# Forgetting attention reordered: head pairs begun among the key tiles, two heads' values side by side, gates copied raw, turned tiles in full banks, norm sums in four groups

## The reference

```python
proj = h @ w_in                                   # h: normed x, (512, 1024)
u_glu, q, k, v, f_logit, gate_c, gate_a = split(proj)
u = depthwise_conv31(a * sigmoid(gate)) + dw_b    # 512 channels, from u_glu
conv_out = silu(layernorm(u, ln_g, ln_b)) @ pw_w
logf = log_sigmoid(f_logit + fox_bf)              # (512, 8)
c = cumsum(logf)                                  # per head
s = q @ k.T / 8 + c_i - c_j ; causal mask         # per head, 512 x 512
attn = softmax(s) @ v                             # 8 heads
merged = sigmoid(gate_c) * conv_out + sigmoid(gate_a) * (attn @ attn_branch_w)
x = x + merged @ w_out
```

## Time and profile before

| what | value |
|---|---|
| median of three runs | 1825.19 us (1824.74 to 1825.5) |
| span of the profiled execution | 1825.3 us |
| PE busy in it | 1712.9 us (94%) |
| VectorE, ScalarE busy | 721.0 us, 409.8 us |
| queries to `pw` (1148.80 to 1347.61 us) | 198.81 us, PE busy 184.50, mean granted clock 0.93 |
| one round of a pair (1269.00 to 1299.72 us) | 30.72 us |

### The profile page before, as it was taken

How to read it: one execution, slowest core, us unless ns; L and a number is a source line. 1 busy time by engine, 2 the same in 40 slices (tenths; PEclk the granted TensorE clock), 3 DMA queues, 4 the chain that set the end, 5 groups by cost and what they waited for, 6 DMA issues and landing times. The chain is left out here.

```text
span 1825.3 us, 21471 instructions
## 1 busy us (share of the span) xinstructions
PE 1712.9 (94%) x8587; PEld 960.1 (53%) x8587; DVE 721.0 (40%) x1329; ACT 409.8 (22%) x758; POOL 21.9 (1%) x29
## 2 busy tenths in 40 slices
PE   6998999999999999999999899998899999877987
PEld 4575466568876443444434334443368674453542
DVE  4635424666545011101110229925353424351425
ACT  5112113532123010110100040126531013220112
POOL 0000000000000000000000000000000000000001
PEclk9998999999999999999999999998999999988999
DMA  9411275111325999999999912210112222269974
GB/s 364 154 57 46 71 261 199 46 70 47 138 93 217 418 419 422 427 420 419 420 426 421 382 69 92 92 46 1 46 47 92 93 99 109 81 253 376 327 270 173
DMA packets 88935, 374.35 MB, mean 205 GB/s; under 512 B 9797, under 2 KB 10133, under 8 KB 73749
## 3 DMA queue, kind: packets, MB, share of 16 engines
q1 hardware_dynamic: 82084, 350.14, 49.0%
q10 hardware_dynamic: 3712, 12.06, 1.7%
q0 software_dynamic: 3056, 11.01, 1.6%
HBM read 466.51 MB, written 10.49 MB: 261 GB/s over the span
## 5 line engine op out<-in xcount | busy, mean ns | idle before, releaser
L2152 PE MATMUL bank<-H,weight_slots 128*128 128x512 f32 (+1 forms) x704 | 290.6, 572 | 4.7 <-ACT H L777 2.9
L2152 PEld LDWEIGHTS bank<-H,weight_slots 128*128 128x128 f32 x704 | 137.1, 197 | 151.8 <-issue 142.7
L2568 PE MATMUL bank<-weight_slots,SM 128*64 128x512 f32 x640 | 144.0, 595 | 9.4 <-DMA weight_slots<-in_w_up_e 9.4
L2253 PE MATMUL bank<-R,weight_slots 128*128 128x256 f32 x560 | 123.8, 380 | 0.0
L2596 PE MATMUL bank<-weight_slots,SM 128*64 128x512 f32 x384 | 114.7, 609 | 3.4 <-DMA weight_slots<-in_w_down_e 3.4
L2152 PE MATMUL bank<-R 128*128 128x128 f32 (+2 forms) x784 | 106.1, 289 | 9.5 <-DVE R L2004 6.2
L2253 PEld LDWEIGHTS bank<-R,weight_slots 128*128 128x128 f32 x560 | 106.1, 190 | 15.7 <-issue 1.5
L2909 PE MATMUL bank<-weight_slots,SM 128*32 128x256 f32 x1536 | 90.8, 390 | 17.4 <-DMA weight_slots<-in_expert_w_gate 9.8
L2152 PEld LDWEIGHTS bank<-R 128*128 128x128 f32 x784 | 95.8, 197 | 13.7 <-DVE R L2001 6.3
L2568 PEld LDWEIGHTS bank<-weight_slots,SM 128*64 128x64 f32 x640 | 45.5, 137 | 104.1 <-issue 83.9
L1701 DVE TENSOR_TENSOR R<-SM,bank 128x512 f32<-128x512 f32 x16 | 11.0, 688 | 217.7 <-PE bank L2568 217.7
(11 more groups left out here) (506 smaller groups left out, 2122.9 us busy)
## 6 DMA issues: line engine op xcount, KB each, us to landing
weight_slots<-in_expert_w_gate SPq DMA_DIRECT2D x51, 1024.0 KB
weight_slots<-in_expert_w_up SPq DMA_DIRECT2D x51, 1024.0 KB
R<-in_expert_w_down SPq DMA_DIRECT2D x51, 1024.0 KB
weight_slots<-in_w_up_e SPq DMA_DIRECT2D x24, 2048.0 KB, 17.5
weight_slots<-in_w_down_e SPq DMA_DIRECT2D x24, 2048.0 KB, 23.8
weight_slots<-in_w_in SPq DMA_DIRECT2D x18, 2048.0 KB, 9.7
weight_slots<-in_w_gate_e SPq DMA_DIRECT2D x16, 2048.0 KB, 17.0
weight_slots<-in_w_ada SPq DMA_DIRECT2D x12, 2048.0 KB, 10.9
```

What stands on the lines that cost most here:

```text
L2152: ins = nc.tensor.matmul(dst, lhsT, rhs, start=(i == 0), stop=(i == len(pairs) - 1))
L2253: ins = nc.tensor.matmul(bank_half(name, i, half)[:, TC * tile:TC * (tile + 1)], lhs[:, kk, m:m + 128], rhs[:, kk, :], start=(begins and k ...
L2568: ins = nc.tensor.matmul(b[64 * half:64 * half + 64, :], xs[:, 4 * rows + k, 64 * e:64 * e + 64], w[k][:, 512 * half:512 * half + 512], st ...
```

## The change

- **Order of queries and keys (PE).** The forget logits come right after the first query tile (in bank 3), so that VectorE's short steps on them move to earlier places in the convolution. The turn of the log-forgets follows the fourth query tile. Pair 0's decays and first scores come after three key tiles, the fourth key tile after them.
- **Norm sums.** Each of the two sums over channels is now four matmuls of 32 columns, one per channel tile, in four column groups of the array (`column_sums`); ScalarE copies the result out (`norm_part`), and one matmul with a 0/1 column folds the four (`fold_sums`). The first stands around the fourth key tile, the second around pair 1's beginning.
- **Turned tiles.** The 20 turns of a pair fill five banks' worth of 512 columns (groups of two heads' tiles); ScalarE copies five times 512 columns (`turned_probs`), into columns of `H` that are free by then, where it copied eight pieces of 512 to 128.
- **Values.** `attend_values` goes through the key tiles with the two heads alternating, at columns 0 and 64 of the array; before, all of one head came before the other. Tile 1 is split in two pieces.
- **Order of the pairs.** Scores of pair hp+1's blocks 2 and 3 are made between the turns of pair hp. The two gate tiles of a round stand after the values and `decays`. There are two buffers for the copied decays.
- **Gates.** VectorE copies each gate tile raw (`gate_copy`), in its place among the scores; ScalarE takes two sigmoids of four tiles each at the end. The final products of the first block's norm move ahead of pair 3's scores on VectorE.
- SP's list is the same, with one name in it changed: the load of `pw` waits for the last query tile as before.

```diff
...
+KEY_BANKS = (0, 1, 4, 5)
...
-    return ("k2_mm", j + 1) if j < 2 else (("k2b_mm", 1), ("k2c_mm", 1))[j - 2]
+    return ("k2_mm", j + 1) if j < 3 else ("k2c_mm", 1)
+def key_out(j):
+    return ("k2_ev", j + 1) if j < 3 else ("k2c_ev", 1)
+def query_done(j):
+    return ("q2b_mm", j) if j else ("q2_mm", 1)
...
-        ln_std = R7[:, 2048:2048 + T]
-        ln_rstd = R7[:, 2048 + T:2048 + 2 * T]
-        ln_sq = R7[:, 3072:4096].rearrange("p (a n) -> p a n", a=2)
+        ln_sq = R7[:, 1536:3584].rearrange("p (k t) -> p k t", k=KH)
+        ln_part = R7[:, 3584:4096]
+        ln_std = ln_rstd = ln_part
...
-        cb = C0[:, :, :, :].rearrange("p a b c -> p (a b c)")[:, 0:1024].rearrange("p (e n) -> p e n", e=2)
+        cb = [a.rearrange("p (e n) -> p e n", e=2) for a in (C0[:, :, :, :].rearrange("p a b c -> p (a b c)")[:, 0:1024], R6[:, 2560:3584])]
         Pbuf = [SM[:, 0:2560], R6[:, 0:2560]]
-        PT2 = R6[:, 2560:3840]
+        PT2 = [H[:, 2 * g:2 * g + 2, T:T + TC] for g in range(4)] + [R6[:, 3584:4096].rearrange("p (a n) -> p a n", a=2)]
+        PT_GROUPS = (((0, 0),), ((1, 0),), ((0, 2), (1, 2)), ((0, 1), (0, 3)), ((1, 1), (1, 3)))
+        def turned_bank(hp, g):
+            return (6, 7, 4 if hp + 1 < FOX_H // 2 else 0, 6, 7)[g]
+        def gate_bank(j):
+            return 5 - j % 2
+        def turned_pieces(e, t):
+            if t == 0:
+                return [(PT2[e], 0, 512, 1 + e)]
+            if t == 2:
+                return [(PT2[2][:, e, :], 256, 256, 3)]
+            if t == 3:
+                return [(PT2[3 + e][:, 1, 128:256], 384, 128, 4 + e)]
+            return [(PT2[3 + e][:, 0, :], 128, 256, 4 + e), (PT2[3 + e][:, 1, 0:128], 384, 128, 4 + e)]
...
-              ("q2", cols(w2, W2_Q), "q2_mm", 4), ("k2", cols(w2, W2_K), "k2c_mm", 1),
+              ("q2", cols(w2, W2_Q), "q2b_mm", 3), ("k2", cols(w2, W2_K), "k2c_mm", 1),
...
+            def norm_part(product, done, bank):
+                act.wait_ge(*reached(product, 1))
+                act.activation(ln_part, PS[bank][:, :], ACT.Copy).then_inc(sem(done), 1)
...
-            def gate_c(j):
-                act.wait_ge(sem("gcm"), j + 1)
-                act.activation(merged[:, j, :], PS[4 + j % 2][:, :], ACT.Sigmoid).then_inc(sem("gc_ev"), 1)
...
+            def turned_probs(hp):
+                for g in range(5):
+                    act.wait_ge(sem("PT_mm"), 5 * hp + g + 1)
+                    if g == 0 and hp:
+                        act.wait_ge(sem("pv2_mm"), hp)
+                    act.activation(PT2[g], PS[turned_bank(hp, g)][:, :].rearrange("p (a n) -> p a n", a=2), ACT.Copy).then_inc(sem("PT_ev"), 1)
+            def heads_out(hp):
+                act.wait_ge(sem("pv2_mm"), hp + 1)
+                act.activation(q2[:, hp, :], PS[5][:, :], ACT.Copy).then_inc(sem("attn_ev"), 1)
+            def gate_sigmoids(first, last):
+                act.wait_ge(sem("gc_ev"), last)
+                act.activation(merged[:, first:last, :], merged[:, first:last, :], ACT.Sigmoid).then_inc(sem("gc_s"), 1)
...
+            for j in range(3):
+                key_copy(j)
             cb_copy(0)
+            norm_part("lnp_mm", "ln_part", 4)
+            probs(0, (0, 1))
+            key_copy(3)
+            norm_squares()
+            norm_part("lnp2_mm", "ln_part2", 7)
+            cb_copy(1)
+            probs(0, (2, 3))
+            norm_root()
+            probs(1, (0, 1))
+            turned_probs(0)
+            probs(1, (2,))
+            heads_out(0)
+            cb_copy(2)
+            probs(1, (3,))
+            conv_silu()
+            probs(2, (0, 1))
+            turned_probs(1)
+            probs(2, (2,))
+            heads_out(1)
+            cb_copy(3)
+            probs(2, (3,))
+            probs(3, (0, 1))
+            turned_probs(2)
+            probs(3, (2,))
+            heads_out(2)
+            probs(3, (3,))
+            scale_probs(FOX_H * TT - 1)
+            gate_sigmoids(0, 4)
+            turned_probs(3)
+            gate_sigmoids(4, 8)
+            heads_out(3)
...
-            convolve(2, range(25))
+            convolve(2, range(8))
...
+            def gate_copy(j):
+                dve.wait_ge(sem("gcm"), j + 1)
+                nc.vector.tensor_copy(merged[:, j, :], PS[gate_bank(j)][:, :]).then_inc(sem("gc_ev"), 1)
...
+            weigh_scores(0, (0, 1))
+            centre_conv()
+            gate_copy(0)
+            weigh_scores(0, (2, 3))
+            gate_copy(1)
...
+            weigh_scores(1, (2, 3))
+            norm_conv()
+            gate_copy(3)
+            weigh_scores(2, (0, 1))
+            gate_copy(4)
+            weigh_scores(2, (2, 3))
...
+            gate_copy(5)
+            weigh_scores(3, (0, 1))
+            gate_copy(6)
+            weigh_scores(3, (2, 3))
+            sum_recip(FOX_H * TT - 1)
+            gate_copy(7)
...
+            query_tile(0)
+            thin_sum(take(3, "f_v", 1), thin, TT, 8, 4, rowb[0:1, 16:24]).then_inc(sem("f_mm"), 1)
+            for j in range(1, 4):
+                query_tile(j)
+            pe.wait_ge(*reached("f_v", 4))
+            b = take(6, "f_v", 5)
+            for t in range(TT):
+                ins = nc.tensor.transpose(b[0:FOX_H, 128 * t:128 * (t + 1)], f_tok[:, t, :], ident)
+            ins.then_inc(sem("fT_mm"), 1)
...
-                if j == 2:
-                    pe.wait_ge(sem("dw_v"), KH * TAPS)
-                    product(take(4, "ln_v", KH)[:, :], [(ones, cT[:, k, :]) for k in range(KH)]).then_inc(sem("lnm_mm"), 1)
-            b = take(5, "ln_std", 1)
-            for k in range(KH):
-                pe.wait_ge(*reached("ln_sq", k + 1))
-                nc.tensor.matmul(b[:, :], ones, ln_sq[:, k % 2, :], start=(k == 0), stop=(k == KH - 1)).then_inc(sem("lnq_mm"), 1)
...
+            def column_sums(done, bank, copied, src, ready):
+                b = take(bank, copied, 1)
+                for k in range(KH):
+                    pe.wait_ge(*ready(k))
+                    ins = nc.tensor.matmul(b[32 * k:32 * k + 32, :], ones[:, 0:32], src[:, k, :], start=True, stop=True, tile_position=(0, 32 * k))
+                ins.then_inc(sem(done), 1)
+            def fold_sums(copied, bank, s_read, value):
+                pe.wait_ge(*reached(copied, 1))
+                return nc.tensor.matmul(take(bank, s_read, value)[:, :], pick[:, 0:1].broadcast_to([P, P]), ln_part, start=True, stop=True)
...
+            def turn_probs(hp, groups):
+                for g in groups:
+                    b = take(turned_bank(hp, g), "PT_ev", 5 * hp + g + 1)
+                    o = 0
+                    for e, t in PT_GROUPS[g]:
+                        for i in range(t, TT):
+                            c = 1280 * e + 64 * i * (i + 1) + 128 * t
+                            ins = nc.tensor.transpose(b[:, o:o + 128], Pbuf[hp % 2][:, c:c + 128], ident)
+                            o += 128
+                    ins.then_inc(sem("PT_mm"), 1)
+            def attend_values(hp):
+                out_b = take(5, "attn_ev", hp + 1)
+                for t in (0, 2, 1, 3):
+                    for e in range(2):
+                        for src, c, n, turned in turned_pieces(e, t):
+                            pe.wait_ge(sem("PT_ev"), 5 * hp + turned)
+                            dst = out_b[64 * e:64 * e + 64, c:c + n]
+                            if t == 0:
+                                dst = dst.rearrange("p (a n) -> p a n", a=2)
+                            ins = nc.tensor.matmul(dst, V2[:, t, 2 * hp + e, :], src, start=(t == 0), stop=(t == TT - 1), tile_position=(0, 64 * e))
+                ins.then_inc(sem("pv2_mm"), 1)
...
+            for j in range(3):
+                key_tile(j)
+            pe.wait_ge(*reached("c_v", 1))
             pe.wait_ge(*reached("q2_ev", 4))
-            pe.wait_ge(*reached("k2_ev", 4))
-            pe.wait_ge(*reached("c_v", 1))
             decays(0)
             logits(0, (0, 1))
+            column_sums("lnp_mm", 4, "ln_part", cT, lambda k: (sem("dw_v"), KH * TAPS))
+            key_tile(3)
+            fold_sums("ln_part", 4, "ln_v", KH).then_inc(sem("lnm_mm"), 1)
             gate_c(0)
             logits(0, (2, 3))
+            column_sums("lnp2_mm", 7, "ln_part2", ln_sq, lambda k: reached("ln_sq", k + 1))
+            decays(1)
+            gate_c(1)
+            logits(1, (0, 1))
+            fold_sums("ln_part2", 6, "ln_std", 1).then_inc(sem("lnq_mm"), 1)
+            gate_c(2)
             for hp in range(FOX_H // 2):
-                if hp + 1 < FOX_H // 2:
-                    decays(hp + 1)
-                    logits(hp + 1, (0, 1))
-                    gate_c(2 * hp + 1)
-                    logits(hp + 1, (2, 3))
-                    gate_c(2 * hp + 2)
-                else:
-                    gate_c(2 * hp + 1)
+                more = hp + 1 < FOX_H // 2
                 pe.wait_ge(sem("P_ready"), 8 * (hp + 1))
-                out_b = take(5, "attn_ev", hp + 1)
```

(29 more changed lines are left out.)

131 lines of the change are left out of this document (53 added, 78 removed).

## The result

| what | value |
|---|---|
| the changed kernel | 1784.25 us, median of 4 runs (1775.42 to 1789.78) |
| the kernel before, beside it | 1825.35 us, median of 4 runs (1824.74 to 1831.91) |
| ratio, 95% interval | 0.9764 (0.9735 to 0.9794) |
| forecast | 1791.0 us, range 1784 to 1804 |
| profiled execution: its time, its span | 1787.18 us, 1785.4 us |

It is faster, by 41.1 us where 34.3 were forecast: the median lies 6.8 us under the forecast and 0.25 above the low end of the range. The page's part 1 of the kernel after answers to the earlier trace rows: PE's busy time fell by 27 us and the span by 40, so about a third of the gain was time in which PE did nothing.

The account below looks back on a forecast made before the run. TensorE (PE), busy 94% of the span, was taken as the bound; gains of 38.1 us less 3.8 given back net 34.3, so 1825.3 becomes 1791.0 us. Its own range was 1786 to 1797, the 8-in-10 range 1784 to 1804.

Parts of the forecast that it names:

- forget logits: wait, trough: Forget logits moved earlier into bank 3: their 0.7 us wait goes, and the clock trough behind costs 1.7, not 2.4.
- norm sums: Two channel sums in four column groups plus folds take 3.8 us in place of 8.7: gain 4.9.
- turned tiles and values: Turns and values of the four pairs take 5.2 us a pair, both heads' values overlapping: gain 18.2.
- waits ahead of the turns, heads' output: PE's waits of 6.5 us before the turns and 0.7 for the heads' output go: gain 7.2, lower bound 0.
- pair 1's scores: The 2.3 us wait in pair 1's scores goes because a gate tile now stands between: gain 2.3.
- two slow gate tiles: Two gate tiles, slow by 1.7 and 2.4 us behind a wait or short passes, run at full speed: gain 4.1.
- given back: Losses in the stage: two clock troughs in longer short-pass stretches, 3.4 us, and four array shape changes, 0.4.
- (1): Rival: the two heads' values do not overlap on the array, costing 9.6 us, total 1800.6; chance 0.08.
- (2): Rival: VectorE's and ScalarE's order is late, losing 4 us a pair in three rounds, total 1803; chance 0.12.
- (3): Rival: `pw` begins too early for VectorE's sums, so some 5 us return, total 1796; chance 0.08.
- (4): Rival: nothing arrives at the end because later stages stand on loads, total 1825; chance 0.03.
- (5): Rival: slower, the clock stays at 1.2 GHz through the rounds; 1843 with half the stage there; chance 0.04.

Follow-up runs that it names:

- full sums: Changed kernel with the four-group norm sums made full 128-column sums again, four accumulated matmuls each, folds kept: stage 162.53 us against 157.45.

## Why the prediction was right and wrong

The mechanism was right: PE's list sets the end, and what the forecast named went. Taken by kinds of work over the whole stage (each matmul counted to the next one's start, waits apart):

| step | forecast | measured |
|---|---|---|
| forget logits: wait, trough | 1.4 | 0.7 + 0.8 = 1.5 |
| their products themselves | 0 | 0.6 |
| norm sums | 4.9 | 4.6 |
| turned tiles and values | 18.2 | 20.0 |
| waits ahead of the turns, heads' output | 7.2 | 7.2 |
| pair 1's scores | 2.3 | 2.3 |
| two slow gate tiles | 4.1 | 4.1 |
| scores | 0 | 0.2 |
| given back: two troughs | -3.4 | 0 |
| given back: changes of shape | -0.4 | none; full tiles +1.0 |
| sum | 34.3 | 41.4 (by the rows 41.5) |

**The step that failed is the one called given back.** It took two troughs of 1.7 us because "the scores of two blocks, the turns and decays now form longer stretches of short passes than any before". None came: the clock stayed at 1.00 in every round of every kernel without a wait there. Nor did the premise hold. Between two full tiles stand 52 passes now and 48 before, but they take 8.6 us (1245.76 to 1254.36, above) where pair 1 in before took 12.9, from 1289.57 to its next gate tile:

```profile
1302.49 7.13 PE L2152 MATMUL bank<-H,weight_slots 128*128 128x512 f32 x16
```

The row that could have told it was in hand: the first values took 3.84 behind a wait of 1.91, the second, with the same turns ahead and short waits only, 2.37. The gate copies alone in the kernel before show it: with 0.5 us of wait in place of 1.9, the same narrow passes at full clock. The forecast took the waits out of its sum and left the price that came with them in it.

What then decides whether a wait brings a slow place is not settled. Before, 1.91 did in three rounds of three; put in, 2.73 and 4.16 did, 2.19 did not, twice, nor did 3.5 in pieces. And behind the forget logits a slow place comes with no wait at all, in most executions but not all. By the Trainium skill, page "TensorE: Matmul & The Clock Gate", section Part 4: PE-mode transpose, transposes do not bring the high clock on as other matmuls do, which would speak for troughs in the rounds. The trace disagrees: behind the wait of 4.16 us put in, PE did twelve turns and nothing else, and the granted clock went from 0.50 in them to 0.99 in the scores right behind.

Of the two or three stretches at half clock that the forecast expected in the stage one came, the one behind the forget logits, at 1.6 where 1.7 was forecast.

Smaller misses. Turned tiles and values were undersized by 1.8: a pair's turns take 2.42 in place of 2.8, and its values 2.36 in place of 2.4. That the values fit is luck: the forecast took 2.37 for one head and nothing for the second, and with the heads apart one takes 2.04, so that the second adds 0.3. The forget logits' products gained 0.6 because in the kernel before their last passes already ran at half clock, in the trough that the forecast counted from the key tiles on. The full tiles together take 1.0 less, where 0.4 more was expected; the 0.1 for a change of shape is there (full sums, above). Most of the 1.0 hangs on the waits: a gate tile that a wait follows counts 7.13 us, to its end, and one with turns right behind it 6.97, since the next matmul starts 0.16 before its end. Four gate tiles and the fourth key tile had such a wait behind them, so a wait costs PE some 0.16 more than its bracket shows.

The rivals: the heads overlap (1), at 2.36 a pair; apart they take 4.08. The helpers are not late (2): PE has no wait in the rounds, and the last shares of pairs 0, 1 and 2 are ready 3.6, 4.1 and 5.1 us ahead of their turns, where a slack of 4.5 was forecast. For pair 0, with the turns at 1245.76:

```profile
1241.49 0.70 ACT L1090 ACTIVATE SM<-SM,tokg 128x512 f32<-128x512 f32 x1
```

`pw` does not wait for its sums (3): PE has no wait between 1311 and 1340 either. The gain arrives (4): what follows `pw` is as long as before, within what it varies by. The clock does not stay low (5): it is at 1.00 from pair 0's decays to `pw`.

The forecast gave the waits ahead of the turns chiefly to the order of the pairs. That is part of the reason: among the turns, either the order or the raw gates alone leave at most 0.3 us of wait, since each covers for the other, and both undone bring 4.0 back.
